# S5 mixer stage: the sample tokens' recurrence for two channel tiles at a time, and output matrices kept for four tiles

## What is computed

```
def s5_mixer(h, h0_re, h0_im, lam_re, lam_im, log_dt, b_re, b_im, c_re, c_im, d_skip, w_glu, b_glu):
    u = hf.reshape(bsz, t, S5_GROUPS, S5_GROUP)                 # 128 groups of 16 channels
    ab_re, ab_im, bb_re, bb_im = s5_discretize(...)             # bb = f * b, per group 64 states x 16 channels
    bu_re = jnp.einsum("btgc,gpc->btgp", u, bb_re)
    bu_im = jnp.einsum("btgc,gpc->btgp", u, bb_im)
    if h0_re is not None:
        c0_re, c0_im = cmul(ab_re, ab_im, h0_re, h0_im)
        bu_re = bu_re.at[:, 0].add(c0_re)                       # and bu_im
    _, _, s_re, s_im = lax.associative_scan(_s5_combine, (a_re, a_im, bu_re, bu_im), axis=1)
    y = einsum("btgp,gcp->btgc", s_re, c_re) - einsum("btgp,gcp->btgc", s_im, c_im)
    y = y.reshape(bsz, t, D_MODEL) + d_skip * hf
    y = jax.nn.gelu(y, approximate=False)
    out = y * jax.nn.sigmoid(y @ w_glu + b_glu)                 # the GLU product
    return out, s_re[:, -1], s_im[:, -1]
```

## Time and profile before

| what | us |
|---|---|
| median of 3 runs | 3961.18 (3957.25 to 3963.7) |
| the profiled execution | 3958.59 |
| its span, first to last instruction | 3956.8 |
| start of DVE's chain of tile 0 | 45.23 |
| start of DVE's chain of tile 15 | 384.80 |
| first instruction of the GLU product | 419.13 |
| PE / DVE / ACT / POOL busy over the span | 2319.9 / 2874.7 / 459.3 / 1541.0 |

### The profile page before, as it was taken

One profiled execution on the slowest core, in us unless ns is written; L12 is line 12 of the kernel. 1 busy time (PEld: TensorE's weight loads), 2 busy tenths in 40 slices (PEclk: granted clock), 3 DMA queues, 4 the chain that ended last, 5 costly groups with the idle time before them and its releaser, 6 DMA issues.

```text
span 3956.8 us, 32035 instructions
## 1 busy us (share of the span) xinstructions
PE 2319.9 (59%) x9698; PEld 1418.8 (36%) x9698; DVE 2874.7 (73%) x4146; ACT 459.3 (12%) x917; POOL 1541.0 (39%) x2027
## 2 busy tenths in 40 slices
PE   4666899100057787658599766562089873002777
PEld 2333668100022235658466336562056321000222
DVE  6777115999975567897767866777958867998555
ACT  6554021000000001220000001210000000000000
POOL 5999102543433333222323342223433443434332
PEclk8877999555589998879799988886599997556999
DMA  1001235799999999999999999999999999999998
GB/s 70 14 11 52 102 128 191 298 424 403 427 427 427 427 427 381 426 426 426 427 409 414 376 392 425 426 426 426 428 427 423 395 427 392 427 427 427 427 427 364
DMA packets 197416, 1404.63 MB, mean 355 GB/s; under 512 B 21952, under 2 KB 26304, under 8 KB 26768
## 3 DMA queue, kind: packets, MB, share of 16 engines
q0 software_dynamic: 167008, 1215.18, 73.3%
q1 hardware_dynamic: 30000, 187.74, 11.7%
q10 hardware_dynamic: 288, 0.18, 0.0%
HBM read 1399.77 MB, written 3.24 MB: 355 GB/s over the span
## 4 chain that ended last, share of the span: by engine, by line
DMA 50%; DVE 18%; PE 15%; POOL 8%; issue 7%; ACT 1%; POOLq 1%; DVEq 0%; ACTq 0%
DMA arena<-in_u_dram,ixs 27%; DMA arena<-in_v_dram,ixs 23%; DVE arena L1581 12%; PE ps L907 6%; PE ps L647 3%; POOL arena L437 3%; PE ps L687 2%; PE ps L805 2%; DVE ps L1601 1%; POOL arena L440 1%; POOL arena L444 1%; POOL arena L445 1%; POOL arena L503 1%; POOL arena L418 1%; POOL arena L441 1%
## 5 line engine op out<-in xcount | busy, mean ns | idle before, releaser
L907 PE MATMUL ps<-arena 128*128 128x512 f32 x2304 | 1122.7, 621 | 1187.7 <-DVE arena L1591 994.8
L1581 DVE CUSTOM_DVE_ANT_0 arena<-arena,ps 128x2048 f32<-128x2048 f32 x556 | 1255.9, 2284 | 194.6 <-DMA arena<-in_u_dram,ixs 180.8
L907 PEld LDWEIGHTS ps<-arena 128*128 128x128 f32 x2304 | 412.6, 194 | 1868.8 <-issue 1349.8
L1601 DVE SCALAR_TENSOR_TENSOR ps<-arena,ps 128x1024 f32<-128x1024 f32 x564 | 726.3, 1288 | 433.9 <-DMA arena<-in_v_dram,ixs 433.5
L503 POOL DMA_INDIRECT arena<-in_u_dram,ixs x560 | 546.8, 976 | 1035.8 <-DVE arena L1581 989.0
L503 POOL DMA_INDIRECT arena<-in_v_dram,ixs x576 | 554.9, 963 | 946.0 <-PE ps L907 799.2
L805 PE MATMUL ps<-HT,W 128*128 128x160 f32 (+1 forms) x3072 | 410.2, 296 | 76.8 <-ACT arena L1191 33.7
L805 PEld LDWEIGHTS ps<-HT,W 128*128 128x128 f32 x3072 | 405.1, 199 | 96.5 <-issue 80.1
L1591 DVE TENSOR_SCALAR arena<-ident,arena 128x128 f32<-128x128 f32 x576 | 164.8, 286 | 56.2 <-PE ps L907 52.2
L833 PE MATMUL ps<-W,arena 128*128 128x128 f32 x1024 | 124.1, 282 | 42.9 <-DVE arena L1706 16.5
L753 PE MATMUL ps<-HN,arena 128*32 128x256 f32 x512 | 139.5, 439 | 0.0
(11 more groups left out here) (250 smaller groups left out, 2159.3 us busy)
## 6 DMA issues: line engine op xcount, KB each, us to landing
W<-in_slabs_dram SPq DMA_DIRECT2D x168, 1024.0 KB, 10.1
arena<-in_u_dram,ixs POOLq DMA_INDIRECT x576, 16.5
arena<-in_v_dram,ixs POOLq DMA_INDIRECT x576, 16.7
GB<-in_norms_dram POOLq DMA_DIRECT2D x4, 1024.0 KB, 6.1
arena<-in_s_bc_dram SPq DMA_DIRECT2D x32, 128.0 KB, 2.1
X<-in_x_dram SPq DMA_DIRECT2D x3, 1024.0 KB, 10.6
out_y_dram<-HN SPq DMA_DIRECT2D x2, 1024.0 KB, 6.3
arena<-in_keys_dram POOLq DMA_DIRECT2D x1, 1024.0 KB, 5.0
```

The lines of the kernel that those rows point to most:

```text
L907: mm = nc.tensor.matmul(ps[:, 8 - SHARE + b, :], DG[(first + n) % DIAGS], ring[:, r, OWN + BANK * b:OWN + BANK * (b + 1)], start=(n == 0), ...
L1581: V.tensor_tensor_reduce(ring[:, r, :], ring[:, r, :], token, 1.0, 0.0, ALU.mult, ALU.add, AV[:, COL_AT[t] + n:COL_AT[t] + n + 1]).then_in ...
L1601: V.scalar_tensor_tensor(to, row, weight, total, ALU.mult, ALU.add).then_inc(row_used[r], 1)
```

## The change

The samples' work is taken out of the tile and put beside it, two tiles at a time:

- The recurrence: `sample_steps(j, steps)` serves tiles 2j and 2j+1 together, with instructions of 128x64 in place of 128x32. POOL does steps 0 and 1 behind its sum (L465 before, L467 now) of tile 2j+1, and steps 2 and 3 with the two copies behind that of tile 2j+2. Steps now write in place into `BS`, which lies in HN and has two slots of two tiles each.
- The out-part of a tile no longer waits for `s5_bsd` and holds the prompt tokens' products alone. The samples' products of a pair are a part of their own, `s5_sample_part(j)`, which stands in PE's queue behind the out-part of tile 2j+2. It waits for the recurrence of the pair and for the GELU of the pair before.
- ACT applies GELU to the samples of two tiles in one instruction (`gelu_samples`), one tile later.
- c, -c and the skip matrices stay for four tiles (`CB`, `CN`, `DD` with four slots), b has two slots (`BB`). SP issues b one tile ahead of c.
- The hardware loops are gone: all 16 tiles are written out on all engines.

```diff
-        BC = view(8320, 1024).rearrange("p (h c n) -> p h c n", h=2, c=4)
+        BB = view(8320, 512).rearrange("p (h c n) -> p h c n", h=2, c=2)
+        CN = view(8832, 512).rearrange("p (h n) -> p h n", h=4)
+        CB = view(22080, 1024).rearrange("p (h c n) -> p h c n", h=4, c=2)
         BX = view(9344, 256).rearrange("p (c n) -> p c n", c=2)
         BT = view(9600, 256).rearrange("p (c n) -> p c n", c=2)
-        CN = view(9856, 256).rearrange("p (h n) -> p h n", h=2)
-        DD = view(10112, 256).rearrange("p (h n) -> p h n", h=2)
-        BS = view(10368, 512).rearrange("p (h c q b t) -> p h c q b t", h=2, c=2, q=QK, b=SB)
-        BSF = view(10368, 512).rearrange("p (h c n) -> p h c n", h=2, c=2)
+        DD = view(9856, 512).rearrange("p (h n) -> p h n", h=4)
+        BS = hn_flat[:, 5120:6144].rearrange("p (j c q b t) -> p j c q b t", j=2, c=2, q=2 * QK, b=SB)
+        BSF = hn_flat[:, 5120:6144].rearrange("p (j c n) -> p j c n", j=2, c=2)
...
+            def s5_c_tile(k):
+
+                if k >= 4:
+                    sp.wait_ge(s5_ys, (k - 4) // 2 + 1)
+                sp.dma_start(CB[:, k % 4].rearrange("p c n -> p (c n)"), s5_bc[k, :, 2 * P:4 * P]).then_inc(s5_c_in[k % 4], 16)
...
+            def diagonal(k):
+
+                if k >= 4:
+                    pool.wait_ge(s5_ys, (k - 4) // 2 + 1)
+                    pool.sem_inc(pool_go, 1)
...
+            def sample_steps(j, steps):
+
+                pool.wait_ge(s5_bsc, 2 * j + 2)
                 pool.sem_inc(pool_go, 1)
+                tiles = slice(2 * QK * j, 2 * QK * (j + 1))
+                a = [w[:, tiles].unsqueeze(2).to_broadcast([P, 2 * QK, SB]) for w in (abr, abi)]
+                t = [PT[:, n, 0:2 * QK * SB].rearrange("p (q b) -> p q b", q=2 * QK) for n in range(4)]
+                for step in steps:
+                    was = [S0[:, c, tiles, :] if step == 0 else BS[:, j % 2, c, :, :, step - 1] for c in range(2)]
+                    now = [BS[:, j % 2, c, :, :, step] for c in range(2)]
                     for n, (c, e) in enumerate([(0, 0), (1, 1), (0, 1), (1, 0)]):
+                        ins = nc.gpsimd.tensor_tensor(t[n], a[c], was[e], ALU.mult)
                     ins.then_inc(pstep, 1)
                     pool.wait_ge(pstep, st.next())
                     nc.gpsimd.tensor_tensor(t[0], t[0], t[1], ALU.subtract)
                     nc.gpsimd.tensor_tensor(t[2], t[2], t[3], ALU.add).then_inc(pstep, 1)
                     pool.wait_ge(pstep, st.next())
+                    nc.gpsimd.tensor_tensor(now[0], now[0], t[0], ALU.add)
+                    nc.gpsimd.tensor_tensor(now[1], now[1], t[2], ALU.add).then_inc(pstep, 1)
+                    pool.wait_ge(pstep, st.next())
+                    pool.sem_inc(pool_go, 1)
+                if ST - 1 in steps:
+                    for c in range(2):
+                        ins = nc.gpsimd.tensor_copy(SSO[:, c, tiles, :], BS[:, j % 2, c, :, :, ST - 1])
+                    ins.then_inc(s5_bsd, 1)
+                    pool.wait_ge(s5_bsd, j + 1)
...
+            def s5_tile(k):
+
+                if k + 1 < KT:
+                    discrete_b(k + 1)
+                pool.wait_ge(s5_bur, k + 1)
                 nc.gpsimd.tensor_tensor(M[2], M[2], M[3], ALU.subtract).then_inc(s5_wi, 1)
+                if k % 2 == 1:
+                    sample_steps(k // 2, range(0, 2))
+                elif k >= 2:
+                    sample_steps(k // 2 - 1, range(2, ST))
+                if k + 1 < KT:
+                    diagonal(k + 1)
...
+            for k in range(KT):
+                s5_tile(k)
+            sample_steps(KT // 2 - 1, range(2, ST))
...
-                pe.wait_ge(s5_bsd, k + 1)
+                if k > 0:
+                    pe.wait_ge(s5_yg, k)
+                nc.tensor.matmul(ps[:, 5, 0:SEQ], DD[:, k % 4, :], HT[:, k, 0:SEQ], start=True, stop=False,
+                                 skip_group_check=True)
                 for q in range(QK):
                     rows = slice(QC * q, QC * (q + 1))
+                    cr, ci = CB[:, k % 4, 0, rows], CN[:, k % 4, rows]
                     for n, c in enumerate((cr, cr, ci, ci)):
+                        mm = nc.tensor.matmul(ps[rows, 5, 0:SEQ], c, PR[n][:, q, :], start=False, stop=(n == 3),
+                                              skip_group_check=True)
                 mm.then_inc(s5_y, 1)
...
+            def s5_sample_part(j):
+
+                pe.wait_ge(s5_bsd, j + 1)
+                if j > 0:
+                    pe.wait_ge(s5_ysg, j)
+                for e in range(2):
+                    k, out = 2 * j + e, slice(NS * e, NS * (e + 1))
+                    nc.tensor.matmul(ps[:, 7, out], DD[:, k % 4, :], HT[:, k, SEQ:NT], start=True, stop=False,
+                                     skip_group_check=True)
+                    for q in range(QK):
+                        rows, at = slice(QC * q, QC * (q + 1)), NS * (QK * e + q)
+                        for n, c in enumerate((CB[:, k % 4, 0, rows], CN[:, k % 4, rows])):
+                            mm = nc.tensor.matmul(ps[rows, 7, out], c, BSF[:, j % 2, n, at:at + NS], start=False,
+                                                  stop=(n == 1), skip_group_check=True)
+                mm.then_inc(s5_ys, 1)
+
+            s5_in_part(0)
+            for k in range(KT):
+                if k + 1 < KT:
+                    s5_in_part(k + 1)
+                s5_out_part(k)
+                if k >= 2 and k % 2 == 0:
+                    s5_sample_part(k // 2 - 1)
+            s5_sample_part(KT // 2 - 1)
+
+            pe.wait_ge(s5_ysg, KT // 2)
...
+            def gelu_samples(j):
+                act.wait_ge(s5_ys, j + 1)
+                A(YT[:, 2 * j:2 * j + 2, SEQ:NT], ps[:, 7, 0:2 * NS].rearrange("p (k n) -> p k n", k=2), ACT.Gelu
+                  ).then_inc(s5_ysg, 1)
```

More of the change, by code:

```diff
@@ L420, in discrete_b @@
                 pool.wait_ge(pstep, st.next())
-                if not first:
+                if k > 0:
                     pool.wait_ge(s5_bt, k)
@@ L442, in sample_states @@
                     pool.wait_ge(pstep, st.next())
-                    s = [BS[:, h, c, :, :, step] for c in range(2)]
-                    nc.gpsimd.tensor_tensor(s[0], s[0], t[0], ALU.add)
-                    ins = nc.gpsimd.tensor_tensor(s[1], s[1], t[2], ALU.add)
-                    if step < ST - 1:
-                        ins.then_inc(pstep, 1)
-                        pool.wait_ge(pstep, st.next())
-                        pool.sem_inc(pool_go, 1)
-                ins.then_inc(s5_bsd, 1)
@@ L451, in sample_states @@
-                pool.wait_ge(s5_bsd, k + 1)
-                pool.sem_inc(pool_go, 1)
-                for c in range(2):
-                    ins = nc.gpsimd.tensor_copy(SSO[:, c, bass.ds(k * QK, QK), :], s[c])
-                ins.then_inc(pstep, 1)
-                pool.wait_ge(pstep, st.next())
[L458 to L462, removed]
-                pool.wait_ge(s5_bur, 2 * i + h + 1)
-                nc.gpsimd.tensor_tensor(M[2], M[2], M[3], ALU.subtract).then_inc(s5_wi, 1)
-                sample_states(i, h)
-                if not last:
-                    if not first:
-                        pool.wait_ge(s5_y, 2 * i + h)
-                        pool.sem_inc(pool_go, 1)
-                    diagonal(*nxt)
+                    nc.gpsimd.tensor_tensor(now[0], now[0], t[0], ALU.add)
@@ L1071, in _ @@
             turns(1)
-            s5_tile(0, 0, first=True, reuse=False)
-            s5_tile(0, 1, reuse=False)
-            with act.Fori(1, KT // 2 - 1) as i:
-                ast.enter(i - 1, 4)
-                s5_tile(i, 0)
-                s5_tile(i, 1)
-            ast.leave(KT // 2 - 2)
-            s5_tile(KT // 2 - 1, 0)
-            s5_tile(KT // 2 - 1, 1, last=True)
+            for k in range(KT):
+                s5_tile(k)
             gelu_y(KT - 1)
+            gelu_samples(KT // 2 - 1)
             with act.Fori(0, 4) as g:
@@ L1439, in _ @@
             dve.wait_ge(norm_tp, 12)
-            s5_tile(0, 0, first=True)
-            s5_tile(0, 1)
-            with dve.Fori(1, KT // 2 - 1) as i:
-                st.enter(i - 1, 4)
-                s5_tile(i, 0)
-                s5_tile(i, 1)
-            st.leave(KT // 2 - 2)
-            s5_tile(KT // 2 - 1, 0)
-            s5_tile(KT // 2 - 1, 1, last=True)
+            for k in range(KT):
+                s5_tile(k)
             final_states(KT - 1)
             dve.drain().then_inc(s5_sf, 1)
-            dve.wait_ge(s5_y, KT)
+            dve.wait_ge(s5_ys, KT // 2)
             with dve.Fori(0, 4) as g:
```

168 lines of the change are left out of this document (66 added, 102 removed).

## The result

The changed kernel takes 3909.3 us (median of 4 runs, 3907.62 to 3912.56) against 3961.8 us before (4 runs): a ratio of 0.987 (1.3% less), 95% interval 0.9853 to 0.9887. The forecast was 3910. The profiled execution took 3912.56 us with a span of 3910.7.

A forecast was written before the change was run, and what follows sets the result against it. POOL bounds the S5 stage, DVE next; periods from 339.57 to 293.3 us gain 46.3, the stage's end 3.5, together 49.8, giving 3908.8, or 3911.4 with the runs' median 2.6 above the profiled one; 3910 taken, range 3893 to 3934.

The forecast's parts named there:

- The bound moves from POOL to DVE: S5 stage: POOL's work per tile falls from 42 to 25 instructions, so DVE becomes the bound; chance 0.72.
- POOL is just ready: POOL in each S5 tile: ready for the next sum at 18.6 or 19.2 us, needed at 18.9 to 19.6.
- The period: DVE's chain per S5 tile: 19.6 us in place of 22.64, in a range of 18.9 to 20.8.
- The price of the wider instructions: DVE beside POOL's 128x64 instructions: about 2 ns per column, 0.06 us at some 12 meetings, 0.7 us per tile.
- The first period: DVE's chain in tile 0, which has no samples' work: 18.9 us.
- The end of the stage: From DVE's last start to the GLU product: 30.8 us against 34.3, gain 3.5, between 0 and 6.
- The sum: S5 stage's periods and end together: gain 46.3 + 3.5 = 49.8 us, from 3958.59 to 3908.8 us.
- PE's and ACT's loop: Out-part, transposes and ACT up to GELU: 14.7 or 18.0 us, mean 16.3 against 19.6, so it stays hidden.
- the new wait on POOL: PE's samples' part waits for POOL's steps 2 and 3, ready at about 16, needed at 21.3: 5 us of room.
- POOL still the bound: Rival: wide POOL instructions cost 0.5 us in the free stretch, period 20.6 to 20.8, time 3924 us; chance 0.19.
- DVE blocked for whole POOL instructions: Rival: DVE loses each POOL instruction's full length, 2.9 us more per tile, period 21.8, time 3940 us; chance 0.04.
- The slower and the unchanged outcomes: Rivals: POOL's steps so late that PE and DVE wait, 4012 us, 0.03; gain given back behind the stage, 0.02.

The follow-up runs named there:

- the early sum with the skip matrix on ACT: Changed kernel with DVE's two products for the sum made first, POOL's sum ahead of `discrete_b`, skip matrix made by ACT: 3898.58 us, ratio 0.9844.

## Why the prediction was right, point by point

- **The bound moves from POOL to DVE.** Right: DVE has no wait left, and taking the whole recurrence away leaves the period at 19.65.
- **POOL is just ready.** Right, but 0.6 to 0.7 us later than reckoned. Forecast were 18.6 and 19.2 us after zero, where zero is the end of L1422. By the timeline, POOL is done 19.15 us after it in the tile shown first (206.89 - 187.74) and 19.90 in the next (227.33 - 207.43), against a next zero at 19.69 and 19.81. The step that slipped: I took the moment from which POOL runs freely, 14.2, from tile 0, but the wider instructions on DVE move it, to 15.1 (202.83 - 187.74). POOL gets 8 through under the scans and not 7, which gives back part. That the 0.1 us of lateness in the second tile costs nothing is because the sum starts under L1424. The run with all steps in odd tiles shows what not being ready costs.
- **The period.** 19.6 forecast, (339.86 - 64.64) / 14 = 19.66 measured after the first. The price of the wider instructions, 0.06 us at each of some 12 meetings, was nearly right: the products went from 1.20 to 1.27 us, the scans from 0.66 to 0.73. In the 13 equal periods it is 19.75, so 0.84 over the 18.91 of tile 0 and not 0.7; the last period, 18.54 us for want of L1405, which the forecast didn't single out, hides most of that in the mean. For the scans, the way to the price was off: 32 columns don't lengthen a scan at all (0.66 us beside them and 0.66 beside nothing), so the 0.16 us of a 128-column one is the price of 128 columns, 1.3 ns for each, and not of 96.
- **The first period.** Wrong by 0.9 us: I took 18.91 because tile 0 has no samples' work. It took 19.79, since the 128-column instructions moved up beside the scans (816 ns each).
- **The end of the stage.** 30.8 us forecast, 28.2 measured. The samples' part takes 1.3 us (366.08 to 367.39) and not 3.3; the out-part 7.8 (358.35 to 366.15) and not 8.4. I had priced the small products at 0.29 us for four records, as they stood between the large ones; in a row, 16 take 0.35 us. POOL's end, forecast at 25 us after DVE's last start, came at 26.1, and the samples' part waited 0.4 us for it.
- **The sum.** 49.8 us forecast to the GLU product, 51.1 measured there, of which 0.4 lie before DVE's first start. The first period took 0.9 more than forecast, the other 14 together 0.8 more, and the end 2.6 less: the near hit of the sum is partly owed to errors of both signs. So is the 3910: the working itself arrives at 3911.4, and the 1.4 us less have no reason given.
- **Hidden parts.** PE's and ACT's loop, the new wait on POOL and the loads: right. The samples' part begins 5.0 us after POOL's copies end (229.36 and 224.34 us in one tile), where 5 was forecast, and with the order on PE reversed the out-part came 4.9 us later in even tiles without an effect. The loops at 0: right, 0.9995 (0.9985 to 1.0005).
- **The rivals.** POOL still the bound fell with the run without the recurrence. DVE blocked for whole POOL instructions fell with the spacing of 1.27 us, where that rule as I read it needed more than 1.4. The Trainium skill, page "SBUF — State Buffer", section "SBUF: two separate sides", gives the pair of ports to whoever is first for its whole instruction. For the 1024-column sum the trace comes close to it (2.07 of 2.35 us); for 64 columns it doesn't, since DVE loses 0.13 us to an instruction of 0.32, and the measurement decides. The slower and the unchanged outcomes needed POOL late or a give-back behind the stage; neither shows.

That the sum is worth moving was not in the prediction. It kept the 2.07 us as a part of 18.91 that I took for DVE's own floor, and it was the next thing to take. The best versions run are the sum on DVE (3897.51 us) and the early sum with the skip matrix on ACT (3898.58); both are about 0.3% faster than the changed kernel (0.9844 of the kernel before, against 0.987).

## What to carry to other kernels

When two engines share a path, go through one period place by place and count how many instructions of the helper fit under each instruction of the other; the count, not the helper's busy share, tells whether it is ready in time, and merging narrow instructions pays where each costs one of the other's turns. What an instruction costs the bound engine goes with its width: short ones are cheap, a long one costs nearly its whole length, and it can be better to let the bound engine do that work itself. A neighbour taken away is replaced by the next in its queue, so ask what moves up.

## What was not expected of the hardware

- DVE's delay by a POOL instruction isn't its length. A product of DVE loses 0.06 us to 32 columns (of 0.25), 0.13 to 64 (of 0.32) and 0.21 to 128 (of 0.40); a scan loses nothing to 32, 0.07 to 64, 0.16 to 128, and 2.07 to 1024 (of 2.35). That is 1.6 to 2 ns per column for a product, less for a scan beside short ones, and some 0.2 to 0.3 us of each POOL instruction in which DVE goes on.
- The other way round there is no such remainder: beside DVE's instructions with two inputs in SBUF, POOL gets one instruction through for each, whatever its width (four in 4.71, 4.90 and 5.24 us with 32, 64 and 128 columns), and beside those that read PSUM it isn't held up at all (0.32 us).
- Taking 16 of 25 POOL instructions per tile away changed the bound engine's period by 0.02 us, because wider ones moved up beside the scans.
